# First modulation by blocks of 512 columns, and the SSM input summed as its channel blocks come, in a one-core Hymba layer

## The chip, the cores and the metric

One core of one Trainium2 chip. TensorE (PE) multiplies, VectorE (DVE), ScalarE (ACT) and GpSimd (POOL) do the rest, SyncE (SP) only starts transfers; ACT starts some too. The metric is device microseconds of one execution, median of several runs, here 1568.83 us (1567.05 to 1568.91). All data are float32.

## What is computed

One layer on 256 tokens of 2048 channels (reference, cut):

```python
mod = silu(c) @ w_ada + b_ada            # 2048 x 12288, six parts of 2048
shift1, scale1, gate1, shift2, scale2, gate2 = split(mod, 6)
h = rms_norm(x, norm1_g) * (1 + scale1) + shift1
p = h @ w_in                             # 2048 x 4096: conv value, conv gate, ssm_in, ssm gate
y_conv = conformer_conv(value, gate)     # GLU, causal conv of 31 taps, layer norm over channels, swish
y_ssm = s5_ssm(ssm_in, gate)             # 64 groups of 16 channels, 64 complex states each, scan over tokens
y = concat(rms_norm(y_conv), rms_norm(y_ssm)) @ w_out
x = x + gate1 * y
x = x + gate2 * hier_moe(rms_norm(x) * (1 + scale2) + shift2)   # 32 experts of 2048 x 512, top 2 of 8 in one of 4 groups
out = rms_norm(x, final_norm_g)
```

## The kernel before

All weights go through a ring of 12 buffers of 1 MB ("units"), filled by SP in the order of use; SP waits on the count `consumed` before it fills a buffer again, and PE waits on `landed` of the buffer. There are four stages. A (36 units) makes the first modulation and the first chunk of the SSM input. B (92 units) makes the other modulation parts and the other seven chunks of `h @ w_in`, with the SSM and the convolution beside them. C (16 units) is `@ w_out` and the router. D is the expert stage, 384 units or more.

A modulation unit (`ada_unit`, L526) is 128 rows of all 2048 columns of one part, rows of 8 KB: four products in the four column groups of the array (L531), each on 512 columns. A `w_in` unit (`chunk_unit`, L547) is four row groups by 512 columns, rows of 2 KB: 16 products (L561) of 256 tokens. Each product has two records in the trace. The six modulation parts come out as rows spread over partitions and are turned into columns by DVE (L1434, L1437) or POOL (L1267 to L1284).

Stage A, in PE's order: 16 units of scale1 (L568); among them the transposes of x (L536), which need x normalised (`x_normed`), of the convolution weights, of the SSM's B matrices and of the router weights. DVE forms scale1 and multiplies hT by it (L1446). Then the four units of chunk 0 (the first 512 channels of the SSM input) are multiplied with hT that lacks the shift, while 16 units of shift1 pass (L605 to L626) with the transposes of the SSM blocks. The shift's share of chunk 0 is made afterwards (L632 to L643): shift1 times the same four units, turned into columns, added when ACT stores the chunk (L1077). DVE adds the shift to hT (L1493).

ACT starts the small transfers. The C matrices come in rows of 256 bytes (L1000, L1001) right behind the squares of x (L998), then the router weights, and only then follows the square root (L1013) that x's normalisation waits for.

Stage B runs in steps g = 4 to 31, one `w_in` unit and two or three modulation units each (`B_LIST`). After each step `side(g)` (L658) puts in what the tables `DRIVE_AT`, `READ_AT`, `SUM_AT` give: for each of eight quads of SSM states a drive (L669, from uT) and a read (L681, L684, to the output), and sums over channels for the layer norm (L656). DVE follows one list written out by hand (L1595 to L1608): quads 0 to 3, the convolution of both halves (L1561, 31 taps by 8 tiles), then quads 4 to 7 with the steps of the conv's layer norm put inside quads 4, 5 and 6. A quad (L1502) reads its drive from PSUM (L1516, L1517), scans (L1529), and turns the states (L1542 to L1545). Quads 4 to 7 need the second chunk of the SSM input, which is chunk 5 of eight. Stage C begins with out unit 0 (L733), which waits for all eight `yc_ready` (L1592), for all chunks and all parts.

Of the kernel before, what the change touches and what calls it, by code (L numbers as in the profile page):

```python
# [31 lines left out]
P = 128  # L32
# [29 lines left out]
A_UNITS, B_UNITS, C_UNITS, D_UNITS = 36, 92, 16, 48  # L62

SCALE, CHUNK_0, SHIFT = 0, 16, 20


def ring_use(n):

    if n < A_UNITS:
        if CHUNK_0 <= n < SHIFT:  # L70
            return 8 + n - CHUNK_0, 0
        n = n - 4 if n >= SHIFT else n
        return n % 8, n // 8
    r, s = divmod(n - A_UNITS, RING)
    return s, r + (4 if s < 8 else 1)


def turn(n):

    if CHUNK_0 <= n < SHIFT:  # L80
        return n + KD
    return n - 4 if SHIFT <= n < A_UNITS else n


D_BASE = A_UNITS + B_UNITS + C_UNITS
# [3 lines left out]
D_USES = [13 if s < 8 else 10 for s in range(RING)]  # L89


CHUNKS = [(2048, "u"), (1024, "gate"), (0, "value"), (1536, "gate"), (512, "value"), (2560, "u"),
          (3072, "out_gate"), (3584, "out_gate")]
FIRST_TILE = [0, 0, 0, 4, 4, 4, 0, 4]
U_CHUNKS, VALUE_CHUNKS = (0, 5), (2, 4)
ADA_PARTS = [2, 3, 4, 5]


DRIVE_AT = [4, 5, 7, 8, 24, 26, 28, 30]
READ_AT = [7, 8, 10, 11, 28, 30, 32, 34]  # L100
SUM_AT = [25, 27, 29]
SIDE_STEPS = 35


def side_jobs(g):


    return [("drive", q) for q in range(QUADS) if DRIVE_AT[q] == g] + \
        [("read", q) for q in range(QUADS) if READ_AT[q] == g] + \
        [("sum", n) for n in range(3) if SUM_AT[n] == g]  # L110


def tile_stored(q):

    return 2 * U_CHUNKS[q // 4] + (q % 4) // 2 + 1


def trunk(nc, a, out):

    ctx = ExitStack()  # L120
    with ctx:
# [26 lines left out]
        sgT = at(56, 8 * KB).rearrange("p (c t) -> p c t", c=CT_)  # L148
# [3 lines left out]
        cst = at(48, 4 * KB).rearrange("p (c q s) -> p c q s", c=2, q=QUADS)  # L152
        cexp = at(52, 8 * KB).rearrange("p (c q g s) -> p c q g s", c=2, q=QUADS, g=2)
        cwst = at(60, 4 * KB, TAPS + 1)
        vst = at(64, P, 40)
        prm = at(98, 20 * P, 32).rearrange("p (n s) -> p n s", n=20)
        btmp = at(108, 4 * KB).rearrange("p (n f) -> p n f", n=2)
# [3 lines left out]
        sq = at(32, 8 * KB).rearrange("p (c t) -> p c t", c=CT_)  # L161
# [27 lines left out]
        bada1 = at(64.5, 2 * KD).rearrange("p (m k) -> p m k", m=2)  # L189
        g1 = at(64.75, KD)  # L190
# [16 lines left out]
        chunk_shift = tiny[:, 8:12]  # L207
        thirty_second = tiny[:, 12:13]
        odd = tiny[:, 6:8]
        cwT = at(65, 256).rearrange("p (c t) -> p c t", c=CT_)  # L210

        par = at(112, 4 * PAIRS).rearrange("p (n q) -> p n q", n=4)
        iota_i = at(112.5, P).bitcast(I32)
        steps = at(113, HALF)
        part_i = at(113.5, 1).bitcast(I32)
# [34 lines left out]
        wr_early = at(90, KD * (NG + EXP)).rearrange("p (k e) -> p k e", k=KD)  # L250
# [23 lines left out]
        x_landed = sem("x_landed")  # L274
        c_landed = sem("c_landed")
        setup_landed = sem("setup_landed")
        wr_landed = sem("router_weights_landed")
# [14 lines left out]
        x_stored = sem("x_transposes_stored")  # L292
# [10 lines left out]
        params_turned = sem("ssm_params_turned")  # L303
        params_stored = sem("ssm_params_stored")
# [13 lines left out]
        scaled_x = sem("x_scaled")  # L318
        shift_ready = sem("shift1_ready")
        shift_rows = sem("shift_rows_done")  # L320
        shift_rows_kept = sem("shift_rows_kept")
        shift_columns = sem("shift_columns_done")
        shift_kept = sem("shift_columns_kept")
# [83 lines left out]
        w_in = a["w_in"][0].rearrange("(p k) n -> p k n", k=KD)  # L407
# [10 lines left out]
        B_LIST, PART_END = [], []  # L418
        ada = 0
        for g in range(4, 32):  # L420
            if g > 4:
                B_LIST.append((g, "in", g // 4, g % 4))
            for _ in range(3 if g < 20 and g % 2 else 2):
                B_LIST.append((g, "ada", ada // KD, ada % KD))
                ada += 1
                if ada % KD == 0:
                    PART_END.append(g)
            if g == 4:
                B_LIST.append((g, "in", g // 4, g % 4))
# [11 lines left out]
        def _(sp):  # L441
            sp.dma_start(ccol[:, :], col(a["c"][0])).then_inc(c_landed, 16)
            sp.dma_start(xr[:, 0, :], a["x"][0, 0:P, :]).then_inc(x_landed, 16)
            sp.dma_start(xr[:, 1, :], a["x"][0, P:T, :]).then_inc(x_landed, 16)
            last_user = {}

            def start(n, s, dst, src):

                if s in last_user:
                    sp.wait_ge(consumed, turn(last_user[s]) + 1)  # L450
                last_user[s] = n
                sp.dma_start(dst, src).then_inc(landed[s], 16)

            def w_in_unit(n, chunk, k):

                s, _u = ring_use(n)
                c0 = CHUNKS[chunk][0]
                start(n, s, ring[:, s, :].rearrange("p (k n) -> p k n", k=4), w_in[:, 4 * k:4 * k + 4, c0:c0 + N])

            for n in range(A_UNITS):  # L460
                if CHUNK_0 <= n < SHIFT:
                    if n == CHUNK_0:
# [1399 lines left out]
```

## Time and profile before

| | us |
|---|---|
| median of the runs | 1568.83 |
| the profiled execution, its time | 1569.61 |
| its span | 1567.8 |
| TensorE busy | 1439.9 (92%) |
| VectorE busy | 524.3 (33%) |
| ScalarE busy | 154.8 (10%) |
| GpSimd busy | 81.1 (5%) |
| moved | 565.45 MB, mean 361 GB/s |
| mean granted TensorE clock | 0.972 |

The page's strip of 40 slices (39.2 us each) shows two regimes. From slice 16 on the transfers run at 421 to 423 GB/s without a gap; that is the expert stage. In the first 15 slices they lie between 55 and 382 GB/s, PE is busy 0.8 to 1.0 from slice 2 on, and DVE is busy 0.8 to 0.9 in slices 4 to 6 and 8 to 11. The clock column is below 0.9 in the first four slices. A line of the timeline gives the start, the duration, the engine, the line and the operation, with the number of instructions merged into it; a bracket gives the idle time of the engine ahead and what ended it. A line of the windows gives the stretch, its length, the busy time of each engine with its instructions, the granted clock (1.00 is 2.4 GHz, 0.50 is 1.2 GHz), the share and the rate of the transfers. A name with q (ACTq, SPq, PEq) is the sequencer of the engine; for a transfer the duration is the time that issuing took.

### The profile page before, as it was taken

How to read it: one execution, taken by the hardware profiler on the slowest of the kernel's cores; microseconds unless marked ns; L12 is line 12 of the kernel's file. 1: busy time of each engine (PE TensorE's matmuls, PEld its weight loads, DVE VectorE, ACT ScalarE, POOL GpSimd, SP SyncE). 2: the span in 40 equal slices, each digit the busy share in tenths (PEclk: the TensorE clock that was granted, in tenths of full speed). 3: DMA queues.
4: the chain of work that ended last, by engine and by line, in shares of the span. 5: the costliest groups of instructions: out<-in, count | busy, mean ns of one | idle time of the engine just before them, and what ended most of it. 6: DMA issues, size and time to landing. Idle time of an engine off the chain costs nothing.

```text
span 1567.8 us, 18904 instructions
## 1 busy us (share of the span) xinstructions
PE 1439.9 (92%) x7424; PEld 656.7 (42%) x7424; DVE 524.3 (33%) x949; ACT 154.8 (10%) x246; POOL 81.1 (5%) x111
## 2 busy tenths in 40 slices
PE   2698999999889989999999999999999999999977
PEld 0364666666644434343343343333333333333322
DVE  0261998499982222111111111111111111111104
ACT  1204000001310311010010010000000000000001
POOL 0000010103010008000000000000000000000000
PEclk8789999999999999999999999999999999999989
DMA  9889979998619336999999999999999999999993
GB/s 341 311 332 382 381 279 366 379 369 329 221 55 375 134 111 235 422 421 421 422 422 422 422 422 422 422 422 422 422 422 423 422 422 422 422 421 422 422 420 127
DMA packets 100848, 565.45 MB, mean 361 GB/s; under 512 B 13064, under 2 KB 13200, under 8 KB 38400
## 3 DMA queue, kind: packets, MB, share of 16 engines
q1 hardware_dynamic: 95744, 559.98, 88.3%
q10 hardware_dynamic: 5056, 4.81, 1.1%
q8 instruction: 33, 0.54, 0.1%
q14 instruction: 15, 0.12, 0.0%
HBM read 562.62 MB, written 2.13 MB: 360 GB/s over the span
## 4 chain that ended last, share of the span: by engine, by line
PE 51%; DVE 15%; DMA 11%; issue 10%; PEld 8%; PEldq 2%; ACT 1%; ACTq 1%; SPq 0%; POOL 0%; DVEq 0%
PE ps L842 19%; PE ps L876 15%; DMA ring<-in_exp_w_down 10%; PE ps L814 7%; PE ps L896 6%; PEld ps L561 4%; DVE arena L1561 3%; DVE arena L1529 3%; PEld ps L733 2%; DVE arena L1517 1%; DVE arena L1516 1%; PEld ps L524 1%; PEldq L737 1%; PE ps L524 1%; DVE arena L1545 1%
## 5 line engine op out<-in xcount | busy, mean ns | idle before, releaser
L842 PE MATMUL ps<-ring,arena 128*64 128x512 f32 x2048 | 458.2, 593 | 11.3 <-DMA ring<-in_exp_w_up 7.7
L842 PEld LDWEIGHTS ps<-ring,arena 128*64 128x64 f32 x2048 | 154.7, 137 | 287.6 <-issue 285.7
L876 PE MATMUL ps<-ring,arena 128*64 128x512 f32 x1024 | 244.4, 602 | 21.3 <-DMA ring<-in_exp_w_down 9.1
L561 PE MATMUL ps<-arena,ring 128*128 128x256 f32 x1024 | 234.0, 388 | 6.1 <-DVE arena L1446 2.9
L561 PEld LDWEIGHTS ps<-arena,ring 128*128 128x128 f32 x1024 | 196.1, 194 | 52.8 <-issue 26.0
L1763 DVE TENSOR_TENSOR arena<-arena,ps 128x512 f32<-128x512 f32 x72 | 49.5, 687 | 277.7 <-PE ps L896 262.9
L876 PEld LDWEIGHTS ps<-ring,arena 128*64 128x64 f32 x1024 | 72.1, 137 | 163.0 <-issue 154.7
L814 PE MATMUL ps<-arena 128*64 128x256 f32 x1024 | 123.4, 385 | 6.4 <-issue 3.8
L531 PE MATMUL ps<-ring,ccol 128*32 128x512 f32 x768 | 100.3, 638 | 23.4 <-DMA ring<-in_w_ada 21.8
L733 PE MATMUL ps<-ring,arena 128*128 128x512 f32 x256 | 111.7, 594 | 0.1
L1737 DVE TENSOR_SCALAR arena<-ps,mod 128x256 f32<-128x256 f32 x64 | 34.8, 544 | 228.4 <-PE ps L814 228.4
L896 PE MATMUL ps<-arena 128*64 128x512 f32 x448 | 106.6, 595 | 2.9 <-issue 1.9
L814 PEld LDWEIGHTS ps<-arena 128*64 128x64 f32 x1024 | 73.0, 138 | 69.8 <-issue 41.8
L1561 DVE SCALAR_TENSOR_TENSOR arena<-arena 128x256 f32<-128x256 f32 x240 | 95.2, 483 | 0.0
L733 PEld LDWEIGHTS ps<-ring,arena 128*128 128x128 f32 x256 | 48.1, 190 | 59.7 <-issue 59.3
L1751 DVE TENSOR_TENSOR arena<-arena,ps 128x512 f32<-128x512 f32 x16 | 11.0, 687 | 177.9 <-PEq L848 176.7
L1744 DVE TENSOR_TENSOR arena<-ps,arena 128x512 f32<-128x512 f32 x64 | 44.3, 692 | 62.0 <-PEq L882 62.0
L1187 ACT ACTIVATE arena<-ps,mod 128x256 f32<-128x256 f32 x64 | 36.1, 564 | 278.8 <-PE ps L814 278.8
L524 PE MATMUL ps<-ident,arena 128*128 128x128 f32 (+3 forms) x276 | 41.2, 282 | 24.2 <-DVE arena L1387 22.2
L896 PEld LDWEIGHTS ps<-arena 128*64 128x64 f32 x448 | 32.0, 137 | 70.1 <-issue 70.1
L524 PEld LDWEIGHTS ps<-ident,arena 128*128 128x128 f32 (+3 forms) x276 | 30.6, 163 | 64.5 <-issue 37.6
L531 PEld LDWEIGHTS ps<-ring,ccol 128*32 128x32 f32 x768 | 20.3, 112 | 69.4 <-issue 60.1
(264 smaller groups left out, 595.1 us busy)
## 6 DMA issues: line engine op xcount, KB each, us to landing
ring<-in_exp_w_gate SPq DMA_DIRECT2D x128, 1024.0 KB, 19.7
ring<-in_exp_w_up SPq DMA_DIRECT2D x128, 1024.0 KB, 18.5
ring<-in_exp_w_down SPq DMA_DIRECT2D x128, 1024.0 KB, 22.4
ring<-in_w_ada SPq DMA_DIRECT2D x96, 1024.0 KB, 9.4
ring<-in_w_in SPq DMA_DIRECT2D x32, 1024.0 KB, 9.1
ring<-in_w_out SPq DMA_DIRECT2D x16, 1024.0 KB, 11.3
arena<-in_x SPq DMA_DIRECT2D x2, 1024.0 KB, 10.1
arena<-in_x SPq DMA_DIRECT2D x1, 2048.0 KB, 10.3
```

The lines of the kernel that those rows point to most:

```text
L524: return nc.tensor.transpose(dst, src, ident[0:k, 0:k])
L531: last = mm(ps[32 * j:32 * j + 32, bank, :], ccol[:, k:k + 1].to_broadcast([P, 32]), ring[:, s, j * N:(j + 1) * N], start=(k == 0), stop=( ...
L561: last = mm(ps[:, j // 2, (j % 2) * T:(j % 2 + 1) * T], ring[:, s, kk * N + j * P:kk * N + (j + 1) * P], hT[:, k, :], start=(k == 0 and j ...
L733: last = mm(ps[:, OUT_BANKS[c][t], :], src[:, k0 + kk, t * P:(t + 1) * P], ring[:, s, kk * N:(kk + 1) * N], start=first, stop=end, skip_gr ...
L814: last = mm(ps[half, 6 + k % 2, 0:T], x1p[:, t, k, half], pick[:, t, :], start=(t == 0), stop=(t == 1), skip_group_check=True)
L842: last = mm(ps[64 * x:64 * x + 64, stage, :], xT[:, k, slot:slot + SLOTS], ring[:, s, kk * N:(kk + 1) * N], start=(k == 0), stop=(k == KD ...
L876: last = mm(ps[half, 2 + n, :], hidT[pr][:, u, half], ring[:, (m + x) % RING, n * N:(n + 1) * N], start=(u == 0), stop=(u == 3), skip_grou ...
L896: last = mm(ps[64 * x:64 * x + 64, 6 + t, :], wpickT[:, pr, t * P + 64 * x:t * P + 64 * x + 64], yexp[pr][:, n, :], start=(pr == 0), stop= ...
L1529: V.tensor_tensor_scan(z, m, z, init, ALU.mult, ALU.add).then_inc(vec_order, 1)
L1561: ins = V.scalar_tensor_tensor(conv[:, c, :], z, cwT[:, c, j:j + 1], conv[:, c, :], ALU.mult, ALU.add)
L1744: V.tensor_tensor(yexp[pr][:, n, :], ps[:, 2 + n, :], gate2[:, n * N:(n + 1) * N], ALU.mult).then_inc(down_stored, 1)
L1763: V.tensor_tensor(acc[:, t, cc], acc[:, t, cc], ps[:, bank, :], ALU.add).then_inc(added, 1)
```

## The change

- Stage A has 40 units, listed in `A_LIST`: scale1 and shift1 in blocks of 512 columns, four units each (rows of 2 KB), and behind each block the two `w_in` units of the 1024 SSM input columns for the 512 channels that the block makes ready (rows of 4 KB). After block b both parts, DVE multiplies and adds on four k tiles of hT in one operation. The eight `u` units sum into four PSUM banks. The later correction by the shift is gone, and the whole SSM input stands at the end of A.
- The 512 columns of a block are turned into channel columns by a copy on ACT (`column_copy`) and four small products (`columns`), as the shift's share was before; h's channels are now in the order of `(k p)`.
- The C matrices come as 128 rows of 2 KB each; POOL doubles them into `cexp`, and the permutation is done by ACT when it stores the blocks (`keep_read`, two copies for each bank). norm1's gain and the first two bias parts come as rows and are turned on PE with the other small vectors. Two transfers of short rows (g2, bada) move behind the column copies.
- On ACT the squares of x come behind the SSM parameters and the router weights' transfers; the square root follows them at once; the B and C matrices' transfers come after it. On DVE the SSM parameters come ahead of x's variance. The stores of x's transposes are split between ACT and DVE.
- Stage B has 88 units in 24 steps: 24 `w_in` units in another order (conv gate 1, value 1, gate 0, value 0, two of the output gate) and 64 modulation units; side jobs stand in half steps (slots).
- DVE's list: quads 0 to 4, convolution of half 1, quads 5 and 6, convolution of half 0, the layer norm's mean, variance and scaling, quad 7 with the last part of the norm inside.
- In each quad `-1` times the state and the product with sin become one operation for each of two halves.

```diff
+A_LIST = [("scale", 0, i) for i in range(4)] + [("shift", 0, i) for i in range(4)]
+for _b in range(3):
+    A_LIST += [("scale", _b + 1, 0), ("scale", _b + 1, 1), ("u", _b, 0), ("scale", _b + 1, 2), ("scale", _b + 1, 3),
+               ("u", _b, 1)] + [("shift", _b + 1, i) for i in range(4)]
+A_LIST += [("u", 3, 0), ("u", 3, 1)]
+CHUNKS = [(1536, "gate", 4), (512, "value", 0), (1024, "gate", 0), (0, "value", 0), (3072, "out_gate", 0), (3584, "out_gate", 4)]
-DRIVE_AT = [4, 5, 7, 8, 24, 26, 28, 30]
-READ_AT = [7, 8, 10, 11, 28, 30, 32, 34]
-SUM_AT = [25, 27, 29]
+DRIVE_AT = [0, 1, 4, 7, 10, 13, 27, 29]
+READ_AT = [3, 7, 9, 13, 15, 29, 32, 49]
+SUM_AT = [42, 44, 47]
...
+            def column_unit(n, kind, b, i):
+                bank = 6 if kind == "scale" else 7
+                if b and i == 0:
+                    pe.wait_ge(col_kept, 2 * b - (kind == "scale"))
+                s = arrived(n)
                 for j in range(4):
+                    k = 4 * i + j
+                    last = mm(ps[32 * j:32 * j + 32, bank, :], ccol[:, k:k + 1].to_broadcast([P, 32]),
+                              ring[:, s, j * N:(j + 1) * N], start=(i == 0), stop=(i == 3), skip_group_check=True)
+                last.then_inc(consumed, 1)
+                if i == 3:
+                    pe.drain().then_inc(ada_done, 1)
+            def columns(x):
+                pe.wait_ge(ada_copied, x + 1)
+                for j in range(4):
+                    last = mm(ps[:, 6 + x % 2, j:j + 1], modrow[:, j * P:(j + 1) * P], thirty_second, start=True, stop=True)
+                last.then_inc(col_done, 1)
+            def u_unit(n, b, i):
...
+                def tiles(pair, kk):
+                    k = 4 * b + 2 * i + kk
+                    pe.wait_ge(h_ready, k + 1)
+                    for j in range(2):
+                        o = kk * CH + (2 * pair + j) * P
+                        last = mm(ps[:, U_BANKS[pair], j * T:(j + 1) * T], ring[:, s, o:o + P], hT[:, k, :],
+                                  start=(k == 0 and j == 0), stop=(k == KD - 1), skip_group_check=True)
+                    return last
...
+                    for k in range(4 * b, 4 * b + 4):
+                        V.tensor_scalar(hT[:, k, :], hT[:, k, :], mod[:, 1, k:k + 1], mod[:, 0, k:k + 1], ALU.mult,
+                                        ALU.add).then_inc(h_ready, 1)
...
-                (cst[:, 0, :, :], a["ssm_c_re"][0].rearrange("(q g) h s -> (g h) q s", q=QUADS)),
+                (cst[:, 0:8, :], a["ssm_c_re"][0].rearrange("g (hh h) s -> (g hh) h s", hh=2)),
...
-                link(V.tensor_scalar(r2[:, :, 0:T], r1[:, :, 0:T], -1.0, None, ALU.mult))
-                link(V.tensor_tensor(r2v[:, :, 0:2, :], r2v[:, :, 0:2, :], s2, ALU.mult))
+                for x in range(2):
+                    link(V.scalar_tensor_tensor(r2v[:, :, x, :], r1v[:, :, x, :], -1.0, sinT[:, 4 * q:4 * q + 4, :], ALU.mult,
+                                                ALU.mult))
...
-            for q in range(4):
+            for q in range(5):
                 quad(q)
-            convolve(0)
-            convolve(1)
+            convolve(1, 0)
+            quad(5)
+            quad(6)
+            convolve(0, 1)
             add_tiles(conv)
-            quad(4, centre)
+            centre()
             add_squares(1)
-            quad(5, scale_conv)
-            add_squares(2)
-            quad(6, norm_conv)
-            quad(7)
+            scale_conv()
+            quad(7, finish_conv)
```

## Rows read from the trace of the kernel before

**Rows 1.** Windows: busy of PE, PEld, DVE, ACT, POOL; clock; DMA share; GB/s
```profile
0.00:144.70 144.70, 94.78 (x569) 51.40 (x569) 43.48 (x87) 28.54 (x36) 3.72 (x13) 0.82 0.89 337
144.70:448.00 303.30, 289.36 (x1782) 199.69 (x1781) 259.60 (x476) 39.09 (x54) 35.89 (x32) 0.99 0.85 323
448.00:592.30 144.30, 130.21 (x377) 59.85 (x373) 51.24 (x106) 23.54 (x41) 7.50 (x15) 0.96 0.50 181
592.30:1567.80 975.50, 925.59 (x4704) 345.80 (x4704) 170.02 (x283) 63.63 (x116) 33.97 (x51) 0.99 0.97 402
```
**Rows 2.** Windows, a stretch in which only rows of 2 KB are fetched
```profile
485.00:500.00 15.00, 15.00 (x36) 6.51 (x35) 4.83 (x10) 0.00 (x0) 0.00 (x0) 1.00 1.05 387
```
**Rows 3.** Timeline of ACT's squares and issues, and the normalisation on DVE
```profile
15.08 1.91 ACT L998 ACTIVATE ring<-arena 128x2048 f32<-128x2048 f32 x1 [11.40 <-DMA arena<-in_x]
...
17.38 18.28 ACTq L1003 DMA_DIRECT2D arena<-in_ssm_c_im  x1
...
35.69 10.52 ACTq L1011 DMA_DIRECT2D arena<-in_router_group_w  x1
...
50.35 2.48 DVE L1387 TENSOR_SCALAR arena<-arena,rstd 128x2048 f32<-128x2048 f32 x2
```
**Rows 4.** Timeline of PE, first modulation unit
```profile
18.05 1.94 PE L531 MATMUL ps<-ring,ccol 128*32 128x512 f32 x8 [18.05 <-DMA ring<-in_w_ada]
```
**Rows 5.** Windows, a stretch of stage A with small transposes and modulation units
```profile
75.00:80.00 5.00, 5.00 (x37) 3.08 (x40) 0.92 (x2) 0.00 (x0) 0.00 (x0) 0.64 1.04 415
```
**Rows 6.** Timeline of PE: costs of the kinds of work
```profile
65.98 3.73 PE L524 MATMUL ps<-ident,arena 32*128 32x32 f32 x32
...
143.78 1.05 PE L642 MATMUL ps<-arena,modrow 128*128 128x1 f32 x8 [0.93 <-DVE modrow L1490]
...
184.73 2.78 PE L531 MATMUL ps<-ring,ccol 128*32 128x512 f32 x24
187.44 1.15 PE L669 MATMUL ps<-arena 32*128 32x256 f32 x16
188.52 0.70 PE L681 MATMUL ps<-arena,skip 128*128 128x256 f32 x2
...
191.01 7.17 PE L561 MATMUL ps<-arena,ring 128*128 128x256 f32 x32
```
**Rows 7.** Timeline of DVE: quads, convolution, layer norm
```profile
157.81 2.29 DVE L1516 TENSOR_TENSOR arena<-ps,arena 128x2048 f32<-128x2048 f32 x1 [9.38 <-PE ps L669]
...
171.60 0.69 DVE L1542 TENSOR_SCALAR arena<-arena 128x1024 f32<-128x1024 f32 x1
172.32 1.23 DVE L1543 TENSOR_TENSOR arena<-arena 128x1024 f32<-128x1024 f32 x1
...
177.17 2.29 DVE L1516 TENSOR_TENSOR arena<-ps,arena 128x2048 f32<-128x2048 f32 x1
...
243.96 47.60 DVE L1561 SCALAR_TENSOR_TENSOR arena<-arena 128x256 f32<-128x256 f32 x120
...
364.91 3.73 DVE L1570 TENSOR_REDUCE arena<-arena 128x256 f32<-128x2048 f32 x1
...
436.64 3.25 DVE L1592 SCALAR_TENSOR_TENSOR arena<-arena,vT 128x256 f32<-128x256 f32 x8
```
**Rows 8.** Timeline of ACT, the square inside the layer norm
```profile
384.65 1.91 ACT L1101 ACTIVATE arena<-arena 128x2048 f32<-128x2048 f32 x1 [12.95 <-DVE arena L1575]
```
**Rows 9.** Timeline of PE: first out unit, the stall behind it, first expert product
```profile
448.06 14.00 PE L733 MATMUL ps<-ring,arena 128*128 128x512 f32 x32
465.62 1.19 PE L681 MATMUL ps<-arena,skip 128*128 128x256 f32 x2 [3.56 <-DVE arena L1545]
...
592.29 8.03 PE L814 MATMUL ps<-arena 128*64 128x256 f32 x58 [2.60 <-DVE arena L1725]
```
**Rows 10.** Timeline of POOL, an operation on 512 elements beside the convolution
```profile
352.12 13.60 POOL L1269 TENSOR_TENSOR modrow<-modrow,own 128x512 f32<-128x512 f32 x1 [35.98 <-ACT modrow L1033]
```

More of the change, by code:

```diff
@@ L414, in col @@
             return v.rearrange("(p k) -> p k", k=KD)
[L418 to L429, printed above, removed]
+        B_LIST = []
+        for g in range(STEPS_B):
+            for n in range(ADA_FIRST[g], ADA_FIRST[g + 1]):
+                B_LIST.append((g, "ada", n // KD, n % KD))
+            B_LIST.append((g, "in", g // 4, g % 4))
         assert len(B_LIST) == B_UNITS
@@ L454, in w_in_unit @@
[L454 to L462, printed above, removed]
-                        sp.wait_ge(x_squares, TT)
-                    w_in_unit(n, 0, n - CHUNK_0)
-                    continue
-                s, _u = ring_use(n)
-                part, k = (1, n) if n < CHUNK_0 else (0, n - SHIFT)
-                start(n, s, ring[:, s, :], w_ada[k, :, part * D:(part + 1) * D])
+            for t in range(TT):
+                sp.dma_start(xr[:, t, :], a["x"][0, t * P:(t + 1) * P, :]).then_inc(x_landed[t], 16)
@@ new lines, in a_unit @@
+            def a_unit(n):
+                kind, b, i = A_LIST[n]
+                if kind == "u":
+                    u_unit(n, b, i)
+                else:
+                    column_unit(n, kind, b, i)
+            pe.wait_ge(c_silu, 1)
+            a_unit(0)
+            a_unit(1)
+            a_unit(2)
+            pe.wait_ge(consts_ready, 1)
+            for g in range(4):
+                turn_x(g)
+            a_unit(3)
+            for g in range(4, 8):
+                turn_x(g)
+            a_unit(4)
@@ new lines, in _ @@
+            turn_small()
+            a_unit(5)
+            columns(0)
+            turn_router(0)
+            a_unit(6)
+            turn_router(1)
+            a_unit(7)
+            turn_b()
+            columns(1)
+            for n in range(8, 14):
+                a_unit(n)
+            turn_blocks(0)
+            turn_blocks(1)
+            columns(2)
+            a_unit(14)
+            a_unit(15)
+            turn_blocks(2)
+            turn_blocks(3)
+            a_unit(16)
+            a_unit(17)
@@ new lines, in _ @@
+            turn_blocks(4)
+            columns(3)
+            turn_blocks(5)
+            for n in range(18, 21):
+                a_unit(n)
+            turn_blocks(6)
+            for n in range(21, 24):
+                a_unit(n)
+            turn_blocks(7)
+            columns(4)
+            for n in range(24, 28):
+                a_unit(n)
+            columns(5)
+            for n in range(28, 34):
+                a_unit(n)
+            columns(6)
+            for n in range(34, 38):
+                a_unit(n)
@@ new lines, in _, with ada_unit @@
+            columns(7)
+            a_unit(38)
+            a_unit(39)
+            def ada_unit(n, i, k):
+                if k == 0:
+                    if i:
+                        pe.wait_ge(ada_copied, 8 + i)
+                    else:
+                        pe.wait_ge(chunk_stored, 1)
+                s = arrived(n)
+                for j in range(4):
+                    last = mm(ps[32 * j:32 * j + 32, 2, :], ccol[:, k:k + 1].to_broadcast([P, 32]), ring[:, s, j * N:(j + 1) * N],
+                              start=(k == 0), stop=(k == KD - 1), skip_group_check=True)
+                last.then_inc(consumed, 1)
+                if k == KD - 1:
+                    pe.drain().then_inc(ada_done, 1)
@@ L1087, in _, with side @@
+            def side(slot):
+                for job, q in side_jobs(slot):
                     if job == "read":
```

677 lines of the change are left out of this document (337 added, 340 removed).

## Prediction

> **What bounds the kernel now.** I read the busy time by stretches first, then the timeline of PE, then those of ACT and DVE. The last stretch [rows 1] is the expert stage: 975.5 us with the transfers at a share of 0.97 and 402 GB/s. The change touches nothing in it, and its ring is full when it starts. So the change is worth exactly what it moves the first expert product, which starts at 592.29 [rows 9]. Before that no transfer bounds for long (shares 0.89, 0.85 and 0.50), so what counts is who is late in each of three stages.
>
> Stage A ends at 144.7. PE is busy 94.8 us of it, at a mean clock of 0.82 [rows 1]. What opens it late is x: the squares start at 15.08, then ACT's queue is held 18.28 us by the second C matrix and 10.52 us by the first router transfer, and x is normalised only at 50.35 + 2.48 = 52.8 [rows 3]. Stage B lasts 303.3 us with PE busy 289.4 and DVE 259.6 [rows 1]: PE bounds it, DVE is close behind. Stage C runs from 448.06 to 592.29, 144.2 us, of which 3.56 us are a stall of PE ahead of the last read, on quad 7's states [rows 9].
>
> **Stage A after the change.** The two blocks on ACT's queue lie behind the squares today and ahead of the square root. The C matrices now come behind the root and in rows eight times as long, so I take both blocks out: x is normalised at 52.8 - 18.3 - 10.5 = 24.0. The SSM parameters come ahead of it on DVE, but their data are small and first in the queue; I cost them at nothing, since DVE has nothing else until the squares, and at 9 us if they come late (estimate, some thirty small operations).
>
> PE's work behind that moment, at full clock [rows 6]: 29 of the 32 modulation units, 2.78 / 3 = 0.93 each, 26.9 (the first three pass while x is awaited); 8 `u` units of 16 products, like a `w_in` unit 7.17 each, 57.4; 145 transposes (32 of x, 13 small, 36 of the router, 32 of B, 32 of blocks) at 3.73 / 32 = 0.117, 16.9; eight times the four small column products, 1.05 each, 8.4. Sum 109.6. What was taken out, the shift's own pass over chunk 0, isn't in it.
>
> The clock adds to this. The same prices for today's stage A give 32 x 0.93 + 4 x 7.17 + 16.9 + 5.3 for the shift's rows + 1.1 = 81.8, against 94.8 busy: a factor of 1.16. The first unit takes 1.94 instead of 0.93 [rows 4, 6]. In the new order the large products stand among the modulation units from about 50 us on, so I take half of the excess, 1.08, giving 118.4. To it come waits: `columns` of the last blocks stand directly behind the unit that they need (drain, copy on ACT, products, DVE), about 1.5 us each, and small ones at the transposes' banks, together 5. **Stage A ends at 24.0 + 118.4 + 5 = 147.4.** Bounds: factor 1.00, 138.6; factor 1.16 and 9 us of late parameters, 165.
>
> Can the transfers hold it up? 32 units with rows of 2 KB, at 387 GB/s [rows 2], take 2.71 us each; if all 40 units and the two halves of x did, it would be 114 us and the start, so about 120, 27 us ahead of PE. They would bound only below some 320 GB/s. Nothing is charged, 5 us at most.
>
> So stage A costs 2.7 us more than now, but does four `w_in` units more, 28.7 us of PE work that leaves stage B.
>
> **Stage B after the change.** PE: 24 x 7.17 + 64 x 0.93 + 8 drives x 1.15 + 7 reads x (191.01 - 188.52 = 2.49) + 2 for three sums = 260 us [rows 6]. DVE is now longer. From the end of A to the first quad: store, two modulation units, drive 0, 3.3 us. A quad takes 177.17 - 157.81 = 19.36. Its L1542 and L1543, 0.69 + 1.23, become two operations on 512 elements, which I take at 0.69 each (half of 1.23 and a start), so 18.82; bounds 0 and -0.8 us for the edit. Five quads: +97.4. The convolution's first half needs value 1. PE has by then done eight `w_in` units, 21 modulation units, six drives and four reads, 93.8 us, and some 3 us of waits for DVE; with drain, copy and POOL's product that is +99.3 or so, a 2 us gap. Half a convolution is 1.3 + 47.6 = 48.9 [rows 7]: +148.2. Quads 5 and 6: +185.8. Value 0 is ready at about the same time, no gap. Second half: +234.8.
>
> Then the layer norm. Today, from its first sum at 364.91 to the end of its last scaling, 436.64 + 3.25 = 439.9, pass 75.0 us, which hold two whole quads (38.7) and the front of a third (19.36 less its last four operations, 5.5, is 13.8): 22.5 for the norm itself, since its trips to PE and ACT run under the quads [rows 7]. In the new list only quad 7's front lies inside, and only one trip is covered. The others lie bare: the square on ACT, 1.91 [rows 8], the mean there and back, and sums that find PE inside a `w_in` unit, up to 7.17 each. I take 6.4 for these, bounds 4 and 16. Norm: 22.5 + 13.8 + 6.4 = 42.7. **`yc_ready` is complete, and out unit 0 starts, at 147.4 + 277.5 = 424.9.** PE has 260 us of work in these 277.5 and waits some 17, most at the end: it has become the idle engine of this stage, DVE the bound.
>
> POOL: `columns(1)` and `columns(2)` run beside the convolution as today, where one operation took 13.60 us [rows 10]; their results are wanted a step or more later, so nothing is charged. The new copy of C has some 35 us of cover. The two products that DVE waits for (`z_tiles`) run beside a quad's tail instead of an idle DVE. The Trainium skill, SBUF — State Buffer, section "SBUF: two separate sides", holds that an operation of one of the two engines can take the shared port pair for its whole length while "the other fully blocks". By that a product of POOL could wait for one DVE operation; the row of 13.60 agrees that it can be much more than one.
>
> **Stage C.** 144.2 as today, less the stall of 3.56, because out unit 0 now covers quad 7's last operations, plus 1 us for products at half clock behind PE's idle time: 141.7. SP's reload of x waits for read 7, which is now earlier in the stage. Weights are in the ring by then.
>
> **Sum.** First expert product at 424.9 + 141.7 = 566.6 instead of 592.3: -25.7. Span 1567.8 - 25.7 = 1542.1. The profiled execution was 1.8 above its span and 0.8 above the median of the runs: 1543.9, and as a median **1543 us**.
>
> **The rivals.**
>
> *PE at full clock through A.* The factor is 1.00, A ends at 138.6, all the rest follows: 1543 - 8.8 = 1534. Against it: in the stretch from 75 to 80 PE is busy all 5.00 us, and the granted clock is 0.64 [rows 5]. The Trainium skill, TensorE: Matmul & The Clock Gate, section "What's actually happening", says that "the default state is throttled, and activity releases the throttle"; by that a PE that never rests after 24 us would have its full clock soon. The row shows that busy time with small transposes isn't enough, so I give this case 0.12.
>
> *A longer tail of DVE.* The bare trips of the norm cost 16 instead of 6.4, or a half of the convolution waits for its product on POOL: +12, 1555. Nothing in the trace of before shows this order, so 0.15.
>
> *The block on ACT's queue comes back, now ahead of the squares.* The place is the squares of x: five router transfers stand in front of them in the new order, behind eleven other small ones, and SP fills its queue with four times as many rows for each unit. If the queue holds ACT for the same 18.28 + 10.52 us, not only the normalisation but also the squares, 2 x 1.91, come behind it: x is normalised 32.6 us later than I forecast, A ends at 180, and the whole stays 1543 + 32.6 = 1576, slower than now. For it: both holds are real, and the router's was itself one of them. Against: each stood behind some thousand rows of 256 bytes, which are no longer in front. It decides from a hold of 25 us on. Chance 0.10. A hold between 19 and 25 us, or late parameters with the clock at 1.16 and the long tail together, ends within 0.2% of today: 0.07.
>
> *It does what it says but the gain is eaten*: B's 28.7 us saved on PE would be worth nothing if DVE began no sooner. That is in the sum: DVE's first quad starts at 150.7 against 157.81, only 7.1 us sooner, and the other 16 us come from its gaps: it is idle 303.3 - 259.6 = 43.7 us of the present B [rows 1], 13.1 of them ahead of quad 0. Going by PE's busy share alone one would have counted the whole 28.7.
>
> **How the numbers follow.** Forecast, 1532 to 1556: 0.56. Full clock: 0.12. Long tail: 0.15. Same: 0.07. Slower: 0.10. Leaving the last two out, and a little below 1534, the range is 1530 to 1563. A measurement of this kernel can tell about 0.2%, 3 us, from no change. Faster 0.83, same 0.07, slower 0.10.
>
> **What would show it.** `x_normed` near 24, no issue on ACT longer than 3 us ahead of it; the last `u` unit near 147 with the clock near 0.9 over A; quads 18.8 apart; gaps of DVE ahead of the convolution halves of 0 to 3 us; PE idle some 10 us or more ahead of out unit 0 at 425; first expert product at 567, and 975.5 us behind it. The prediction is wrong if the last isn't so (an expert stage that starts with fewer units in its ring), if stage A is bound by transfers, or if the norm's tail is far from 43 us.

## The result and the profile after the change

The changed kernel takes 1559.39 us (median of 5 runs, 1558.76 to 1561.50) where the kernel before took 1568.18 beside it: a ratio of 0.9942, interval 0.9931 to 0.9954. It is faster, by some 9 us; the prediction said 26. The profiled execution has a span of 1559.8 us and a time of 1561.5. The stages, cut at the same events as in [rows 1]:

```profile
0.00:147.20 147.20, 122.94 (x721) 82.27 (x721) 43.46 (x86) 37.68 (x50) 7.30 (x14) 0.92 1.03 375
147.20:438.00 290.80, 261.65 (x1653) 177.23 (x1653) 267.23 (x484) 35.43 (x48) 87.72 (x40) 0.97 0.83 315
438.00:579.30 141.30, 130.80 (x371) 60.30 (x372) 38.92 (x83) 23.15 (x40) 1.94 (x7) 0.96 0.52 186
579.30:1559.80 980.50, 924.64 (x4704) 346.04 (x4704) 170.16 (x283) 63.70 (x116) 34.02 (x52) 0.99 0.96 400
```

Stage A ends 2.5 us later than before, B is 12.5 us shorter, C 3.0 us shorter, and the expert stage D, which the change doesn't touch, is 5.0 us longer. The last is the first surprise; the other is B, where DVE works 267 us of 290.8.

The timeline of PE at the four places that carry the sum: the last `u` products of stage A, the first out unit, the first expert product, and the last job's first `down` product. They answer to [rows 9], the last has no row of before there.

```profile
133.14 14.05 PE L563 MATMUL ps<-arena,ring 128*128 128x256 f32 x64 [0.87 <-DVE arena L1566]
...
437.99 9.59 PE L811 MATMUL ps<-ring,arena 128*128 128x512 f32 x16 [5.73 <-DVE arena L1699]
...
579.30 8.99 PE L890 MATMUL ps<-arena 128*64 128x256 f32 x64 [2.59 <-DVE arena L1837]
...
1501.58 5.11 PE L952 MATMUL ps<-ring,arena 128*64 128x512 f32 x16 [13.50 <-issue]
```

Ahead of the last job PE is idle for 13.50 us, put down to "issue": it waits for no semaphore that the profile shows. The same place of the kernel before:

```profile
1508.61 6.51 PE L876 MATMUL ps<-ring,arena 128*64 128x512 f32 x16 [7.66 <-issue]
```

It stands behind the loops over the experts' jobs, where PE branches past code that isn't run (`pe.If`). The timeline of DVE, first with the beginnings of quads 0 and 1 and of both halves of the convolution, then the layer norm's tail (they answer to [rows 7]):

```profile
150.59 2.29 DVE L1622 TENSOR_TENSOR arena<-ps,arena 128x2048 f32<-128x2048 f32 x1 [16.25 <-PE ps L755]
...
169.40 2.29 DVE L1622 TENSOR_TENSOR arena<-ps,arena 128x2048 f32<-128x2048 f32 x1
...
214.27 4.18 DVE L1635 TENSOR_TENSOR_SCAN arena<-decay,arena 128x128 f32<-128x128 f32 x8
...
249.84 47.59 DVE L1668 SCALAR_TENSOR_TENSOR arena<-arena 128x256 f32<-128x256 f32 x120
...
332.66 4.16 DVE L1652 TENSOR_TENSOR arena<-arena 128x2048 f32<-128x2048 f32 x1
...
338.15 47.60 DVE L1668 SCALAR_TENSOR_TENSOR arena<-arena 128x256 f32<-128x256 f32 x120
385.85 3.79 DVE L1677 TENSOR_REDUCE arena<-arena 128x256 f32<-128x2048 f32 x1
398.19 2.29 DVE L1682 TENSOR_TENSOR arena<-arena 128x2048 f32<-128x2048 f32 x1 [8.55 <-ACT arena L1205]
...
419.04 4.28 DVE L1635 TENSOR_TENSOR_SCAN arena<-decay,arena 128x128 f32<-128x128 f32 x8
...
434.59 3.25 DVE L1699 SCALAR_TENSOR_TENSOR arena<-arena,vT 128x256 f32<-128x256 f32 x8
```

The mean is subtracted at 398.19, and DVE sat idle for 8.55 us ahead of it. The sum that it needs, though, is a product of PE of 389.74, 0.67 us long. What lay between is on the queue of ACT:

```profile
390.63 0.82 ACTq L1233 DMA_DIRECT2D scale_shift_scratch<-mod  x2
397.36 0.38 ACTq L1237 DMA_DIRECT2D arena<-scale_shift_scratch  x1
397.79 0.37 ACT L1205 COPY arena<-ps 128x256 f32<-128x256 f32 x1 [19.65 <-DMA scale_shift_scratch<-mod]
```

ACT takes its instructions in order. It waited first for the third set of modulation columns (until 390.6), issued their two stores, waited until those had landed (397.36), issued the load, and only then copied the mean. And the third set was late because of POOL:

```profile
244.44 3.91 POOL L1410 TENSOR_TENSOR arena<-arena 128x1024 f32<-128x1024 f32 x1 [10.63 <-ACT arena L1194]
...
280.89 17.46 POOL L1387 TENSOR_TENSOR modrow<-modrow,own 128x512 f32<-128x512 f32 x1 [31.16 <-ACT modrow L1181]
...
332.28 2.39 POOL L1410 TENSOR_TENSOR arena<-arena 128x1024 f32<-128x1024 f32 x1 [11.84 <-ACT arena L1194]
...
341.23 45.00 POOL L1380 TENSOR_SCALAR skip<-ident,vT 128x128 f32<-128x128 f32 x1 [6.29 <-PE ps L772]
386.19 1.06 POOL L1387 TENSOR_TENSOR modrow<-modrow,own 128x512 f32<-128x512 f32 x1
...
390.38 0.22 POOL L1401 TENSOR_TENSOR mod<-mod,g 128x16 f32<-128x16 f32 x1
```

The skip matrix of quad 7, a product over 128 elements that took 0.60 us at 319.84, took 45.00 us. It began 3 us into the second half of the convolution and ended with it, at 386.2; `columns(1)`, from 280.89, ended at 298.4, with the first half (297.4). [Rows 10] is the same thing: 352.12 + 13.60 = 365.7, beside a half that ended at 364.9.

### The profile page after: what moved, and what is told of

The parts are those of the page before. It is cut to its first block, busy times and chain, and to the rows that moved or that the text cites. A ratio compares the mean times of both kernels' runs of the same rounds, so it can differ in the third digit from the quotient of the medians.

```text
span 1559.8 us, 18926 instructions
## 1 busy us (share of the span) xinstructions
PE 1440.0 (92%) x7448; PEld 665.8 (43%) x7448; DVE 519.8 (33%) x934; ACT 160.0 (10%) x254; POOL 131.0 (8%) x112
## 4 chain that ended last, share of the span: by engine, by line
PE 62%; DVE 13%; DMA 11%; issue 7%; PEld 4%; PEldq 1%; SPq 1%; ACT 1%; POOL 0%; DVEq 0%; ACTq 0%
PE ps L918 20%; PE ps L952 15%; DMA ring<-in_exp_w_down 10%; PE ps L890 7%; PE ps L972 6%; PE ps L722 3%; DVE arena L1668 3%; PE ps L563 3%; DVE arena L1635 2%; PEld ps L811 2%; PE ps L508 2%; DMA ring<-in_w_ada 1%; PE ps L707 1%; PE ps L524 1%; DVE arena L1623 1%
## 5 line engine op out<-in xcount | busy, mean ns | idle before, releaser
L722 PEld LDWEIGHTS ps<-arena,ring 128*128 128x128 f32 x768 | 146.0, 192 | 36.8 <-issue 17.2
L1380 POOL TENSOR_SCALAR skip<-ident,vT 128x128 f32<-128x128 f32 x8 | 50.9, 6361 | 215.4 <-PE ps L772 212.9
```

The costliest lines, as they stand in the source:

```text
L722: last = mm(ps[:, j // 2, (j % 2) * T:(j % 2 + 1) * T], ring[:, s, kk * N + j * P:kk * N + (j + 1) * P], hT[:, k, :], start=(k == 0 and j ...
L1380: gp_.tensor_scalar(skip[:, :], ident[:, :], vT[:, 4, q:q + 1], None, ALU.mult).then_inc(skip_ready, 1)
```

## The experiments

The profiled executions differ by up to 4 us in where the first quad begins, without a cause that I know (148.5 to 152.5 in the ten with this stage A; 150.6 and 152.2 in two of the same kernel), so that inside stage B I count from the first quad. From it to out unit 0 pass 290.25 us in the kernel before, 287.40 in the changed one, and 274.2 by the prediction. All were timed beside the kernel before, and a ratio is to that.

**ACT's wait.** The edit on ACT:

```diff
-                if g == 19:
-                    act.wait_ge(parts_ready, 3)
-                    ... two stores
-                if g == 20:
-                    act.wait_ge(ab_stored, 32)
-                    ... one load
+            act.wait_ge(parts_ready, 3)
+            ... two stores
             side(49)
+            act.wait_ge(ab_stored, 32)
+            ... one load
```

> The changed kernel with one edit on ACT: the wait for the third set of modulation columns with its two small stores, and the wait for those stores with the load behind it, stand behind the last sum of the layer norm and behind read 7's GELU; no work is left out. Theory (the mean's copy is held by ACT's own queue order): in the changed kernel the sum is ready at 390.4 and its copy comes at 397.79; here it comes at about 390.5, and everything behind it moves up by 7.4 us: out unit 0 at about 430.5, time about 1559.4 - 7.4 = 1552. Rival (the tail is inherently long, POOL or PE would hold the mean for as long): no change, 1559. Third reading (half of it comes back through PE's clock or the columns' late transfers): 1555 to 1557.

Measured: 1553.52 us (six runs from 1552.32 to 1557.81), ratio 0.9914 [0.9901, 0.9927]. The mean's copy in this kernel:

```profile
388.35 0.37 ACT L1205 COPY arena<-ps 128x256 f32<-128x256 f32 x1 [12.33 <-PE ps L740]
```

It now waits for PE's sum, and for nothing else. From the first quad (148.50) to out unit 0 (429.03) pass 280.53 us, 6.9 fewer than in the changed kernel. The theory holds, a little below its 7.4: the mean's copy comes 7.4 us sooner, but the next sum, of the squares, is waited for 0.5 us longer. The medians give 5.9 us; three of the six runs lie at 1554 to 1558, and what set them apart isn't shown.

**What holds POOL.** Two kernels, the first with POOL's order changed:

```diff
-            diagonal(7)
             columns(2)
+            diagonal(7)
```

> The changed kernel with one edit on POOL: the third set of modulation columns stands ahead of the skip matrix of quad 7 in its queue; no work is left out. The skip matrix took 45.00 us beside the second half of the convolution. Theory (whatever operation of POOL starts beside the back-to-back products of the convolution gets no turn until they end; the row for the columns is there at 351.6, inside the half): the first product of the columns takes some 34 us instead and ends with the half too, the third set is ready at about 390, and the time stays 1559.4. Rival (the skip matrix is a single unlucky operation, and the columns beside the convolution would take 5 to 14 us as the two slow ones of the kernel before): the set is ready at 357 to 366, the mean is copied at 390, and the time is 7.4 us shorter, 1552.

Measured: 1561.31 us, ratio 0.9954 [0.9940, 0.9967], and 286.65 us from the first quad to out unit 0: no gain. The first product of the columns took what was forecast for it, and the skip matrix behind it its usual 0.61:

```profile
350.41 34.99 POOL L1387 TENSOR_TENSOR modrow<-modrow,own 128x512 f32<-128x512 f32 x1 [16.75 <-ACT modrow L1181]
...
388.71 0.61 POOL L1380 TENSOR_SCALAR skip<-ident,vT 128x128 f32<-128x128 f32 x1
```

So it isn't this one operation. A second execution of the changed kernel (`e6_after_again` below) says the same: there the skip matrix of quad 6 fell beside the first half and took 47.42 us, and the first product of the third columns, beside the second half, 38.81.

The second kernel leaves POOL alone and gives DVE's stream pauses:

```diff
+                        if j % 3 == 2 and i == 0:
+                            dve.wait_ge(conv_step, done)
```

> The changed kernel with one edit on DVE: at every third tap of the convolution DVE waits until its last product is through, which leaves a short pause, ten in each half; no work is left out, and ACT's and POOL's orders are as in the changed kernel. Theory (POOL is shut out only while DVE's products follow each other without a pause): each pause lets one operation of POOL pass; the skip matrix of quad 7 takes at most 5 us, the eight operations of the third set of columns need a pause each, and the set is ready before the half ends; the mean's copy comes at once behind its sum. The pauses cost DVE about 0.1 us each, 1 us in a half, so -7.4 + 2 = -5.4 us, 1554. Rival (a pause is too short, or POOL's wait has another cause than DVE's stream): the skip matrix takes 45 us as before, and the time is 0 to 2 us longer, 1560 to 1562.

Measured: 1560.49 us, ratio 0.9959 [0.9946, 0.9973]. POOL, then DVE's second half:

```profile
280.47 1.11 POOL L1387 TENSOR_TENSOR modrow<-modrow,own 128x512 f32<-128x512 f32 x1 [30.70 <-ACT modrow L1181]
...
341.80 1.08 POOL L1380 TENSOR_SCALAR skip<-ident,vT 128x128 f32<-128x128 f32 x1 [6.29 <-PE ps L772]
352.26 1.33 POOL L1387 TENSOR_TENSOR modrow<-modrow,own 128x512 f32<-128x512 f32 x1 [9.37 <-ACT modrow L1181]
353.67 2.23 POOL L1390 TENSOR_TENSOR modrow<-modrow 128x256 f32<-128x256 f32 x4
```
```profile
338.73 50.40 DVE L1670 SCALAR_TENSOR_TENSOR arena<-arena 128x256 f32<-128x256 f32 x120
```

The skip matrix takes 1.08 us instead of 45.00, and `columns(1)` 1.11 instead of 17.46: with the pauses the waits are gone, so the uninterrupted stream is the cause. The rest of the expectation missed. A pause costs not 0.1 but 0.28 us (50.40 against 47.60, ten pauses), 5.6 us in both halves together, and this eats the 5.6 us by which the tail (46.5 us from the end of the second half to out unit 0, against 52.1) became shorter.

**The early x alone, in the kernel before.** The root directly behind the squares, the router's transfers behind it, the C matrices, still in rows of 256 bytes, behind the last function of the SSM parameters:

```diff
-            ... two issues of C, five of the router's weights
             act.wait_ge(x_var, 1)
             A(rstd[:, 2:4], rstd[:, 0:2], ACT.Sqrt).then_inc(x_root, 1)
+            ... five issues of the router's weights
             ...
             A(prm[:, 8, :], prm[:, 9, :], ACT.Sin, ...)
+            ... two issues of C
```

> The kernel before with one edit in the order of ACT's issues: the square root of x's variance stands directly behind the squares, the five router transfers behind the root, and the two C matrices (still in rows of 256 bytes) behind the last small function of the SSM parameters, with a semaphore of their own; no work is left out. It separates the early x from the rest of the change. Theory of the prediction's stage A: x is normalised at about 24 instead of 52.8, and what then bounds stage A is PE's 95 us of work behind it or the transfers (0.89 of 144.7 us busy, so no sooner than 129): stage A ends 12 to 18 us sooner, and stages B and C keep their lengths, since PE's chain there is the same: 1568 - 15 = 1553, bounds 1550 to 1557. Rival (the early x is worth little, since the next thing waits: the C matrices' own hold of 18 us falls on ACT's copies or on the blocks that PE turns): 0 to -5, 1563 to 1568.

Measured: 1555.69 us, ratio 0.9922 [0.9909, 0.9935]: with this alone the kernel before is about 12.5 us faster, by the medians more than with the whole change. Its windows, and the issue that held ACT for 18.28 us in [rows 3]:

```profile
0.00:131.10 131.10, 96.95 (x585) 50.53 (x585) 46.97 (x101) 30.32 (x36) 3.72 (x13) 0.88 1.00 377
131.10:434.50 303.40, 290.09 (x1765) 201.08 (x1765) 256.16 (x462) 37.10 (x54) 35.89 (x32) 0.98 0.84 321
434.50:578.70 144.20, 130.18 (x375) 59.71 (x371) 51.11 (x105) 23.53 (x41) 7.45 (x15) 0.96 0.49 182
578.70:1554.00 975.30, 925.89 (x4704) 345.92 (x4704) 170.06 (x283) 63.71 (x116) 34.02 (x52) 0.99 0.97 402
```
```profile
42.60 0.60 ACTq L1028 DMA_DIRECT2D arena<-in_ssm_c_im  x1
```

Stage A is 13.6 us shorter and the other three have their old lengths to 0.2 us. In A the transfers' share is 1.00, but that doesn't make them the bound of the whole stage: PE waited for a unit last at 49.80, 9.9 us in all behind the first one, and SP waited 78.2 us in all for a buffer to come free. So the transfers held PE in the first 50 us, and behind that PE, busy 73.5 of the other 81.1 us, set the length.

**Row size or place.** Against it, the changed kernel with its C matrices (rows of 2 KB) put back in front of the squares:

```diff
+            ... two issues of C
             for t in range(TT):
                 act.wait_ge(x_landed[t], 16)
```

> The changed kernel with the two C matrices (rows of 2 KB, as there) issued on ACT ahead of the squares of x, about where the kernel before had them; the B matrices stay behind the root. No work is left out. In the kernel before the second C matrix held ACT's queue for 18.28 us. Theory (the short rows of 256 bytes, 1024 of them in a matrix, made the hold): each issue takes about 0.45 us, x is normalised 1 us later, and the time stays within 1 us of 1559.4. Rival (the place made it: the queue is full there, whatever the rows are): a hold of 10 to 18 us comes back, x is normalised at 33 to 41, and the time is 1569 to 1577.

Measured: 1559.59 us, ratio 0.9945 [0.9932, 0.9959].

```profile
16.20 0.45 ACTq L1088 DMA_DIRECT2D arena<-in_ssm_c_im  x1
```

No hold. With the row above, the hold is gone in both kernels: with long rows at the early place, and with short rows at 42 us. Neither run shows the cause by itself, since what stands ahead differs too: here the transfers of the B matrices, `g2` and `bada` come later than they did, and in the other kernel the router's stand in front. The time alone isn't it: in the kernel before with the early x the router's first transfer is issued at 17.13 and takes 0.34 us, where it took 10.52 behind the C matrices. Why the queue holds ACT at 17 us with the short rows and not at 42 wasn't tried.

**The idle time ahead of the last job.** The edit, on PE's first line, in the changed kernel (65 waits, 32 instructions more) and in the kernel before (56 waits, 27 more); the numbers of instructions are reckoned at two waits each, which no view shows:

```diff
+            for _ in range(65):
-            pe.wait_ge(c_silu, 1)
+                pe.wait_ge(c_silu, 1)
```

> The changed kernel with 32 more instructions on PE, all of them waits that are long satisfied, at the very start; no work is left out. Only the place of the later code moves. In the changed kernel the branch behind the expert loop leads to code of which one weight load runs at 1496.03 and the rest 5.5 us later, after a second instruction load; the last job's first product stands 13.50 us idle against 7.66 before. Theory (the target of the branch lies one or two instructions ahead of the end of a block of code, so two loads come one after the other): moved by 32 instructions it lies inside the next block, one load is enough, the idle time is 7.5 to 8 us and the time 5.5 to 6 us shorter, about 1553.7. Rival (the 13.50 us come of data, of a semaphore or of the transfers): no change, 1559.

> The kernel before with 27 more instructions on PE, waits that are long satisfied, at its start, so many that the target of the branch behind the expert loop comes to the same place in the code as in the changed kernel; no work is left out. Theory (place of the code): the idle time ahead of the last job's first product grows from 7.66 to about 13.5 us, and the time by 4.5 to 6 us, to 1573 or 1574. Rival (the changed kernel's longer idle time has another cause): 7.7 us and 1568, no change.

Measured: 1555.99 us, ratio 0.9924 [0.9912, 0.9937], for the first; 1571.88, ratio 1.0029 [1.0017, 1.0041], for the second. The changed kernel with the waits, then the kernel before with them:

```profile
1493.88 6.16 PE L953 MATMUL ps<-ring,arena 128*64 128x512 f32 x16 [7.68 <-issue]
```
```profile
1511.49 5.00 PE L877 MATMUL ps<-ring,arena 128*64 128x512 f32 x16 [13.01 <-issue]
```

Waits that hold nothing up, 1490 us earlier, turn 13.50 into 7.68 and 7.66 into 13.01: the place of the code makes the idle time. How it does so shows in PE's weight loads of the changed kernel: one runs at 1496.03, the next 5.37 us later, put down to "issue" again.

```profile
1496.03 0.18 PEld L952 LDWEIGHTS ps<-ring,arena 128*64 128x64 f32 x1 [8.83 <-issue]
1501.58 0.29 PEld L952 LDWEIGHTS ps<-ring,arena 128*64 128x64 f32 x3 [5.37 <-issue]
```

The transfers bear the loads out. In the changed kernel's idle time two packets of 16 KB come on the queue that the trace names "instruction", one between 1492 and 1494 and one between 1498 and 1500; in the kernel before there is one. It is so in all thirteen kernels of this document: two packets in the eight that stand idle 13.0 to 13.5 us, one in the five with 7.5 to 7.7. The queue doesn't name its engine. That the target lies just ahead of the end of a block, so that two loads come one behind the other, fits this; where the block ends is seen in no row.

The medians moved by less than the idle time (3.4 and 3.5 us against 5.8 and 5.4). Stage D by itself, from the first expert product to the end, is 975.6 us instead of 980.5 with the waits in the changed kernel, and 979.3 instead of 975.5 in the kernel before; in all thirteen it is 975.5 to 975.8 or 979.3 to 980.6, by the number of packets. It moved by less than the idle time since the products behind it are slower after the shorter one: 6.16 and 6.51 us for the 16 against 5.11 and 5.00.

**Both edits.** ACT's wait moved and 32 instructions more:

> The changed kernel with both edits tried so far: ACT's wait for the third set of modulation columns and its stores behind the last sum of the norm, and 32 satisfied waits more on PE at its start; no work is left out. If the two costs are separate, they add: -7.4 and -5.5 us, 1559.4 - 12.9 = 1546.5. If the shorter tail only brings the last job's code and data in another order (the two costs overlap), less: 1551 to 1553.

Measured: 1549.56 us (1548.22 to 1553.16), ratio 0.9889 [0.9874, 0.9904], beside 1559.37 (0.9945) for the unedited changed kernel on the same chip: 9.8 us. The two add, as far as the runs can tell (5.9 + 3.4 is 9.3). Of that unedited kernel it had been written:

> The changed kernel itself, unedited, as a baseline on the chip of the other three kernels of this group. Both theories: 0.994 of the kernel before, 1559.4, with the mean's copy 7.4 us behind its sum and 13.5 us of idle time ahead of the last job's first product.

The idle time was 13.30. The mean's copy came at 398.54, only 5.8 us behind the sum, since PE itself came to the sum later here: it ended at 392.70, 1.3 us behind the end of DVE's first sum at 391.41, where it took 0.8 before.

**POOL's products on DVE.** To the kernel with both edits:

```diff
-            z_tiles(1)
-            z_tiles(0)
...
             def convolve(h, turn):
+                dve.wait_ge(chunk_stored, 4 + 2 * (VALUE_0, VALUE_1)[h] + 2)
+                z = zT[:, 4 * h:4 * h + 4, PAD:]
+                V.tensor_tensor(z, z, vals, ALU.mult).then_inc(z_ready, 1)
```

> The kernel with both edits tried before (ACT's wait moved behind the last sum, 32 satisfied waits more on PE) and with the two products of gate and value on DVE itself, directly ahead of each half of the convolution, instead of on POOL; no work is left out. Theory (POOL's products collide with DVE's: one took 3.90 us beside quad 4's tail where 2.18 is its free time, and DVE's last product of quad 6 took 4.15 instead of 2.29 beside the other): DVE does each in about 1.2 us; the first half begins at first quad + 98.5 instead of + 99.2, and the second about 2 us sooner than now, the time is 1 to 2 us shorter, 1548. Rival (DVE's 2.4 us more of work are simply added): 1 to 2 us longer, 1551.

Measured: 1548.34 us, ratio 0.9875 [0.9860, 0.9889]; against the version without it no difference that these intervals can tell. The product on DVE, in a timeline:

```profile
330.23 2.29 DVE L1643 TENSOR_TENSOR arena<-arena 128x2048 f32<-128x2048 f32 x1
332.56 1.23 DVE L1650 TENSOR_TENSOR arena<-arena 128x1024 f32<-128x1024 f32 x1
...
382.86 3.63 DVE L1671 TENSOR_REDUCE arena<-arena 128x256 f32<-128x2048 f32 x1
...
399.74 1.75 DVE L1686 RECIPROCAL arena<-arena 128x256 f32<-128x256 f32 x1 [3.58 <-ACT arena L1212]
```

The last product of quad 6 is back at 2.29 us, and the second half ends 233.87 us behind the first quad instead of 235.21. But out unit 0 comes 280.69 behind the first quad, not 280.47 - 1.3: the sum of the squares stands on PE behind three modulation units, which end at 398.57, and DVE waits 3.58 us ahead of its reciprocal instead of 2.35. The 1.3 us are real and lost 17 us later. By its median it is the fastest version that was run.

**The quad's tail.** The changed kernel with the old pair of operations:

```diff
-                for x in range(2):
-                    link(V.scalar_tensor_tensor(r2v[:, :, x, :], r1v[:, :, x, :], -1.0, ...))
+                link(V.tensor_scalar(r2[:, :, 0:T], r1[:, :, 0:T], -1.0, None, ALU.mult))
+                link(V.tensor_tensor(r2v[:, :, 0:2, :], r2v[:, :, 0:2, :], s2, ALU.mult))
```

> The changed kernel with the old tail of a quad: one negation over 1024 elements and one product over 1024 instead of two combined operations over 512; no work is left out. By the prediction's step this is worth 0.54 us for each quad that lies ahead of out unit 0 on DVE's chain, of which there are seven (quad 7's tail lies behind it): quads 19.35 apart, out unit 0 at 3.8 us later, the time 3.8 us longer, 1563.2. Rival (the tail is hidden beside PE's work): no change, 1559.4.

Measured: 1564.49 us, ratio 0.9979 [0.9970, 0.9988]; quads 19.36 apart, 290.76 us from the first to out unit 0, 3.4 more than in the changed kernel. The medians differ by 5.1, and the 1.7 between the two measures isn't explained. So this small edit is worth 3.4 to 5 of the change's 9 us; DVE bounds stage B, as forecast.

## Why the prediction was wrong

Its direction and its picture of the bounds were right. The step that failed first is the norm's tail: ACT's wait for the third set of columns was charged at nothing. Two more terms were at nothing, POOL's work beside DVE's and the last job's code, and all made it too hopeful. The span was to be 1542.1 and is 1559.8, 17.7 more: +13.1 to out unit 0, -0.4 in stage C, +5.0 in D.

- *Stage A, right.* x is normalised at 23.1 (24.0), no issue on ACT ahead of it takes over 0.7 us, the last `u` products end at 147.2 (147.4), the first quad begins at 150.59 (150.7). From 23.06 to 147.20 PE is busy 117.6 us at a clock of 0.90 (118.4), and idle 6.5 (5). The rival of the returning block didn't come, nor did it with the C matrices in front of the squares as well. The transfers' share is 1.03, but PE waited for a unit last at 33.49, so behind that they didn't bound it. The first quad's start varied by 4 us between executions, so the hit to 0.2 us is partly luck.
- *Quads, right.* 18.81 apart, gap of 2.15 ahead of the first half.
- *From the first quad on.* The prediction took out 16 us of DVE's gaps here, 290.25 to 274.2; 2.9 came, 287.40. The rest of stage B's gain lies ahead of the first quad, which comes 3.4 us behind stage A's end instead of 13.1. The next two points are the 13 us that are missing.
- *The second half of the convolution, 3.8 us too early.* From the first quad to the layer norm's first sum I counted 231.5 us and it took 235.3. POOL's work beside DVE's is 3.4 of it: eight scans of quad 3 took 4.18 instead of 2.63 beside `columns(0)`, the last product of quad 6 took 4.16 instead of 2.29 beside POOL's second `z` product. The step said that POOL's products run "beside a quad's tail instead of an idle DVE", and charged nothing for it.
- *The norm's tail, 9.4 us too short.* 52.1 for 42.7. 7.4 of it at the mean's copy, 6.8 by the tail of the kernel with ACT's wait moved, is the step that failed: "their results are wanted a step or more later, so nothing is charged". It was true of the results' readers and forgot ACT, which waits for the third set in its own queue ahead of the mean's copy; a wait names all that stands behind it. Before, [rows 10], the set was ready 4 us behind the half's end as well, but there the first sum wasn't followed by a bare norm. The rest is the scans of quad 7 beside `columns(3)` (4.28 for 2.63) and longer bare waits: 7.3 us instead of 6.4 in the kernel with ACT's wait moved. These two, 2.6 us, are what its tail of 45.3 lies above 42.7.
- *Stage D, 5.0 us too short.* "The change touches nothing in it" was right of its instructions and wrong of their place: the idle time ahead of the last job grew from 7.66 to 13.50 us, and D was back at 975.6 with the waits on PE. The prediction named this as what would make it wrong, for another reason (the ring).
- *The rival of the longer tail* had its size (+12) and its place right, and its cause, bare trips to PE and ACT, wrong: 7.4 us of it was a wait for two stores that the norm doesn't need.
- *What the change is made of.* The prediction gave the early x no price of its own. By the kernel before with that edit alone it is worth 12.5 us, all of it in stage A. The quad's tail is worth 3.4 to 5. ACT's wait and the place of the code cost 9.8 together. The change as a whole gained 9, so that the blocks, the `u` sums in stage A and the new order are worth 9 - 12.5 - 4.3 + 9.8, some 2 us, without these two costs. This number is a difference of four others, with the early x taken from the other kernel's stage A as if it would add; no run shows it by itself.

The Trainium skill, SBUF — State Buffer, section "SBUF: two separate sides", says of the pair of ports that DVE and GpSimd share that whoever comes first holds it "for the whole instruction", and that "the other fully blocks". That the other is blocked agrees with the traces. The length doesn't go far enough: the skip matrix waited 45 us, at 47.60 / 120 = 0.40 us each through some 113 instructions of DVE (an estimate), not one, and got in as soon as DVE paused. That it is the ports is the page's account; the runs show the stream and the pause.

## What to carry to other kernels

When an operation is moved, ask not only who reads its result but which in-order queue waits for it, and what stands behind that wait. On POOL, count an operation beside a stream of DVE operations like this convolution's (two inputs, no pause) as ending when the stream does, at 128 elements as at 512; a pause in the stream cost 0.28 us here, moving the wait on ACT cost nothing. Try each part of a large change alone: here the order of seven transfers in the old kernel gave, by the medians, more than the whole.

## What the runs showed of the hardware that was not expected

- POOL starved by DVE: 0.60 us became 45.00, 1.06 became 34.99 and 17.46, each ending within 1 us of the end of the stream of `scalar_tensor_tensor`. With a pause at every third tap the same three operations took 1.08, 1.33 and 1.11. In the other direction the loss is small: eight scans 4.2 us for 2.63, a product over 2048 elements 4.16 for 2.29.
- The place of code: behind a branch over code that isn't run, PE stood for 7.5 to 7.7 us with one packet of 16 KB on the instruction queue, or 13.0 to 13.5 with two, and 56 or 65 satisfied waits at the start of the program decided which. Two kernels that differ by nothing else differed by 3.5 us.
- The same issue of a C matrix in rows of 256 bytes held ACT's queue for 18.28 us at 17.38, and 0.60 us at 42.60, with other transfers ahead of it.
